# A two-block model on one core: fused mask and maximum, eight results per PSUM bank, x reloaded later

## The reference

```python
def dsa_attention(q, k, v, iq, ik, iw):       # 8 heads, per block of 128 queries
    ...
    logits = jnp.where(ok[:, :, None, :], logits, -jnp.inf)
    p = jax.nn.softmax(logits, axis=-1).astype(v.dtype)
    ...
def windowed_gqa(u, w_in, sink, w_out):       # 16 heads
    ...
        logits = logits - slopes[:, :, None, None] * dist
        logits = jnp.where(valid, logits, NEG_BIG)
        sink_col = jnp.broadcast_to(sink_l[None, :, :, None, None], logits.shape[:-1] + (1,))
        probs = jax.nn.softmax(jnp.concatenate([logits, sink_col], axis=-1), axis=-1)[..., :-1]
    ...
def second_block(x, p, ...):
    h = x
    for i in range(DEPTH_2):
        u = rms_norm_2(h, norm_g[i])
        ...                                    # y = windowed_gqa(u, ...), then y = mla(u, ...)
        h = h + y
        gate = jax.nn.sigmoid(rms_norm_2(h, ple_norm_g[i]) @ ple_w_gate[i])
        h = h + (p[i] @ ple_w[i]) * gate
    return rms_norm_2(h, final_norm_g)
```

## Time and profile before

| | |
|---|---|
| median of 3 runs | 2800.81 us (2798.86 to 2802.94) |
| the profiled execution | 2798.45 us, its span 2796.6 us |
| busy: PE, DVE, ACT, POOL | 2515.2, 1558.5, 594.7, 1602.1 us |
| chain that ended last | PE 77%, DVE 12%, DMA 3%, issue 2%, ACT 2%, POOL 2% |
| sparse attention | 321 to 381 us |
| gelu stage with gates | 792 to 1176, without them to 1282 |
| down stage | 1285 to 1963 |
| windowed attention | 2084 to 2212 |
| a_out, ple_w0, norm(3), ple_g0, norm(4) | 2223 to 2357 |
| latent attention | 2485 to 2644 |
| b_out, ple_w1, norm(5), ple_g1, norm(6) | 2653 to 2796 |

### The profile page before, as it was taken

The page is one execution under the profiler, slowest core; times in us unless marked ns, Lnnn a source line. Parts: engine busy times, 40 slices in busy tenths (PEclk is TensorE's granted clock), DMA queues, the critical chain, the costliest instruction groups (busy, mean ns, idle before and its releaser), DMA issues.

```text
span 2796.6 us, 38708 instructions
## 1 busy us (share of the span) xinstructions
PE 2515.2 (90%) x12856; PEld 1260.3 (45%) x12856; DVE 1558.5 (56%) x2823; ACT 594.7 (21%) x1243; POOL 1602.1 (57%) x1048
## 2 busy tenths in 40 slices
PE   3767788999999999978999999999898888989987
PEld 1423443444455555433444444444355533557633
DVE  6498583699967777505952222250218836555525
ACT  1111221111122222201111111110125322245412
POOL 4535435799976767659976666660560157830053
PEclk7878898999999999989999999999999999999998
DMA  6216312354446587577765555560220022310021
GB/s 228 98 44 215 118 38 80 113 150 143 146 147 199 179 249 246 166 217 254 261 220 204 201 204 201 204 224 15 84 83 1 9 75 68 106 53 1 9 75 38
DMA packets 189252, 375.45 MB, mean 134 GB/s; under 512 B 13536, under 2 KB 79200, under 8 KB 189152
## 3 DMA queue, kind: packets, MB, share of 16 engines
q1 hardware_dynamic: 119696, 332.64, 35.8%
q10 hardware_dynamic: 69456, 41.49, 5.0%
HBM read 302.77 MB, written 71.30 MB: 134 GB/s over the span
## 4 chain that ended last, share of the span: by engine, by line
PE 77%; DVE 12%; DMA 3%; issue 2%; ACT 2%; POOL 2%; ACTq 1%; SPq 0%; DVEq 0%; POOLq 0%
PE ps L624 65%; PE ps L714 3%; PE ps L734 3%; PE ps L840 2%; PE ps L723 2%; DMA arena<-ada_w 2%; DVE arena L1280 2%; PE ps L672 1%; ACTq L1097 1%; DVE arena L1384 1%; DVE arena L1383 1%; DVE spare L1190 1%; DVE arena L1245 1%; ACT arena L1016 1%; DVE arena L1218 1%
## 5 line engine op out<-in xcount | busy, mean ns | idle before, releaser
L624 PE MATMUL ps<-hT,parts 128*128 128x512 f16 x4800 | 1070.3, 383 | 66.1 <-DVE hT L1198 29.6
L573 POOL TENSOR_SCALAR parts<-ring 128x1024 f16<-128x1024 f32 x261 | 297.9, 1141 | 955.3 <-PE ps L624 890.0
L624 PEld LDWEIGHTS ps<-hT,parts 128*128 128x128 f16 x4800 | 466.5, 98 | 642.0 <-issue 43.3
L624 PE MATMUL ps<-arena 128*128 128x512 f16 x3072 | 666.2, 380 | 8.4 <-DVE arena L1544 8.4
L576 POOL TENSOR_TENSOR parts<-ring,parts 128x1024 f16<-128x1024 f32 x261 | 577.2, 2212 | 21.7
L624 PEld LDWEIGHTS ps<-arena 128*128 128x128 f16 x3072 | 300.9, 98 | 374.5 <-issue 15.0
L1539 DVE TENSOR_TENSOR arena<-arena 128x512 f32<-128x512 f32 x128 | 149.7, 1170 | 451.6 <-DMA arena<-gate_mem 447.8
L574 POOL TENSOR_SCALAR ring<-ring 128x1024 f32<-128x1024 f32 x261 | 306.6, 1175 | 0.0
L594 POOL TENSOR_TENSOR arena<-ring,arena 128x1024 f16<-128x1024 f32 x128 | 283.6, 2215 | 10.6
L592 POOL TENSOR_SCALAR arena<-ring 128x1024 f16<-128x1024 f32 x128 | 148.2, 1158 | 169.7 <-PE ps L624 169.7
L624 PE MATMUL ps<-arena,parts 128*128 128x512 f16 x876 | 199.8, 389 | 49.4 <-POOL parts L576 34.3
(11 more groups left out here) (169 smaller groups left out, 2414.6 us busy)
## 6 DMA issues: line engine op xcount, KB each, us to landing
ring<-w SPq DMA_DIRECT2D x133, 512.0 KB, 3.3
ring<-u SPq DMA_DIRECT2D x128, 512.0 KB, 3.9
ring<-v SPq DMA_DIRECT2D x128, 512.0 KB, 3.4
act_mem<-spare SPq DMA_DIRECT2D x128, 256.0 KB, 4.0
gate_mem<-arena ACTq DMA_DIRECT2D x4, 8192.0 KB, 42.0
arena<-act_mem SPq DMA_DIRECT2D x128, 256.0 KB, 3.6
arena<-gate_mem SPq DMA_DIRECT2D x128, 256.0 KB, 3.8
arena<-ada_w SPq DMA_DIRECT2D x48, 512.0 KB, 4.8
```

Of the source, the lines that this page charges most:

```text
L573: G.tensor_scalar(dst[:, 0, :], src, WS, 1.0, ALU.mult, ALU.mult).then_inc(scaled, 1)
L624: ins = [T.matmul(out_, a, b, start=start and j == 0, stop=stop and j == 2) for j, (a, b) in enumerate(((lhs[0], rhs[0]), (lhs[0], rhs[1]) ...
```

## The change

In the attention (all three kinds):

- mask and maximum are one VectorE instruction with an accumulator. It writes the negated logits and their minimum; the exp is then taken with scale -1. In the windowed kind the logits come already divided by the head's slope (the table `steep`, in the copy of a_q), the instruction multiplies by the slope again, and the negated sink is the minimum's starting value.
- the results of eight units lie side by side in one PSUM bank, and VectorE scales all eight at once; maxima, sums and sinks have a column for each of the eight. Values wait for a scaling only in the first unit of eight, for that of sixteen units back. The sinks' exponentials are done for eight units at once.

x is reloaded behind the last gelu. Beyond that, norms 1 and 3 to 6 have their parts moved into the stage ahead, two blocks behind it; in norms 3 and 5 the last two parts lie behind the second and third block of ple_w0 or ple_w1, and ScalarE's copies of that stage are spread over the norm. Norms 4 and 6 square into `aq`, as `hT` is still being read. A one-element root ahead of the last square loads the table early.

```diff
             def values(u):
                 ...
-                    if u0 + u >= 2:
-                        pe.wait_ge(o_ready, u0 + u - 1)
+                    if u % EIGHT == 0 and u0 + u >= 2 * EIGHT:
+                        pe.wait_ge(o_ready, (u0 + u) // EIGHT - 1)
+                    at = place(un) * 64
...
-            features("a_out", in_parts(az), lambda k: pe.wait_ge(turned_read, t_a + k + 1))
-            features("ple_w0", in_parts(pT), lambda k: pe.wait_ge(p_ready, k + 1))
-            norm(3)
-            features("ple_g0", hr, h_need(3))
-            norm(4)
+            features("a_out", in_parts(az), lambda k: pe.wait_ge(turned_read, t_a + k + 1), behind(3, 2))
+            features("ple_w0", in_parts(pT), lambda k: pe.wait_ge(p_ready, k + 1),
+                     lambda m: norm_part(3, KC - 3 + m) if m in (1, 2) else None)
+            features("ple_g0", hr, h_need(3), behind(4, 2))
+            last_parts(4, 2)
...
+            def square(n, k, need):
+                if k == KC - 1:
+                    own.do(A.activation(warm[:, n:n + 1], eps[:, 0:1], ACT.Sqrt))
+                need(k)
+                own.do(A.activation(squares_of(n)[:, k, :], xT[:, k, :], ACT.Square), squares)
...
-                    if un["kind"] == "window":
-                        own.do(A.activation(sm[:, 8 + u % 4:9 + u % 4],
...
+                    if un["kind"] == "window" and u % EIGHT == EIGHT - 1:
+                        act.wait_ge(sink_shifted, u // EIGHT + 1)
+                        own.do(A.activation(eight_sinks(u), eight_sinks(u), ACT.Exp), sink_exps)
...
+            gelus(AT_GATES + S // GROUP, CHUNKS)
             act.dma_start(xT[:, :, :], x_park.rearrange("c p n -> p c n")).then_inc(x_back, 16)
-            gelus(AT_GATES + S // GROUP, CHUNKS)
...
-            take("a_q", lambda s, b: copy(aq[:, s, :], b, scale=0.125 / WS))
+            act.wait_ge(rows2_loaded, 16)
+            steep = ROWS2["steep"][0]
+            take("a_q", lambda s, b: copy(aq[:, s, :], b, scale=rows2[:, steep + s:steep + s + 1]))
...
+                for s in range(KC + 1):
+                    if s < KC:
+                        take(name, gate, s, s + 1)
+                    if s >= 1:
+                        square(n + 1, s - 1, of_sum)
...
                     elif un["kind"] == "window":
...
-                        own.link(V.scalar_tensor_tensor(out=soft_b[:, u % 2, 0:w], in0=rows2[:, at:at + w],
-                                                        scalar=-slope, in1=src, op0=ALU.mult, op1=ALU.add))
-                        src = soft_b[:, u % 2, 0:w]
-                    ins = V.tensor_reduce(nm, src, AX, ALU.max, negate=True)
...
+                        own.do(V.tensor_tensor_reduce(out=soft_b[:, u % 2, 0:w], in0=src, in1=rows2[:, at:at + w],
+                                                      scale=-slope, scalar=small_w[:, 48 + un["h"]:49 + un["h"]],
+                                                      op0=ALU.add, op1=ALU.min, accum_out=peak(un, u)), max_ready)
...
                 def normalise(u):
+                    if u % EIGHT != EIGHT - 1:
+                        return
...
-                    own.do(V.tensor_scalar(out_rows(un), ps[:, u % 2, 0:64], tot, None, ALU.mult), o_ready)
...
+                        own.do(V.tensor_tensor(out_.rearrange("p (e d) -> p e d", d=64),
+                                               src.rearrange("p (e d) -> p e d", d=64), by, ALU.mult), o_ready)
```

More of the change, by code:

```diff
@@ L452, in soft_buffers, with peak, eight_peaks, total_at @@
             return soft_w, probs_w, probsT_w, small_w
+        def peak(un, u):
+            n = (u // EIGHT % 2) * EIGHT + place(un) + (32 if un["kind"] == "sparse" else 0)
+            return soft_buffers(un["kind"])[3][:, n:n + 1]
+        def eight_peaks(u):
+            n = (u // EIGHT % 2) * EIGHT
+            return small_w[:, n:n + EIGHT]
+        def total_at(un, u):
+            return (u // EIGHT % 2) * EIGHT + {"sparse": 48, "window": 16, "latent": 64}[un["kind"]]
+        def total(un, u):
+            n = total_at(un, u) + place(un)
+            return soft_buffers(un["kind"])[3][:, n:n + 1]
+        def eight_totals(un, u):
+            n = total_at(un, u)
+            return soft_buffers(un["kind"])[3][:, n:n + EIGHT]
+        def eight_sinks(u):
+            n = 32 + (u // EIGHT % 2) * EIGHT
+            return small_w[:, n:n + EIGHT]
         block = ctx.enter_context(nc.Block())
@@ L647, in features @@
                     last.then_inc(summed, 1)
+                    if after is not None:
+                        after(m)
             def tokens(name, lhs, need=None):
@@ L678, in norm, with behind, last_parts @@
                 for k in range(KC):
+                    norm_part(n, k)
+            def behind(n, lag):
+                return lambda m: norm_part(n, m - lag) if lag <= m < KC + lag else None
+            def last_parts(n, lag):
+                for k in range(KC - lag, KC):
                     norm_part(n, k)
@@ L980, in copy, with norm @@
                 return A.activation(dst, src, ACT.Copy, scale=scale)
-            def norm(n, need, shift_of=None):
-                for k in range(KC):
-                    need(k)
-                    own.do(A.activation(hT[:, k, :], xT[:, k, :], ACT.Square), squares)
+            def square(n, k, need):
[3 more added lines that the diff above has]
+                own.do(A.activation(squares_of(n)[:, k, :], xT[:, k, :], ACT.Square), squares)
+            def norm(n, need=None, shift_of=None, between=None):
+                if need is not None:
+                    for k in range(KC):
+                        square(n, k, need)
+                if between is not None:
+                    between(-2)
                 act.wait_ge(norm_sum, n + 1)
@@ L1124, in _, with embedded @@
             attention(units_window(), U_WINDOW)
-            take("ple_w0", lambda s, b: copy(ple[:, s, :], b))
             def ple_gate(name, n):
-                norm(n, x_from("a_out" if n == 3 else "b_out"))
+                def embedded(k):
+                    first, last = {-2: (0, 3), -1: (3, 6), 1: (6, 7), 2: (7, 8)}.get(k, (0, 0))
+                    take("ple_w0" if n == 3 else "ple_w1", lambda s, b: copy(ple[:, s, :], b), first, last)
+                norm(n, x_from("a_out" if n == 3 else "b_out"), between=embedded)
                 def gate(s, b):
@@ L1133, in gate, with of_sum @@
                     return A.activation(gate_t[:, s % 2, :], b, ACT.Sigmoid, scale=1.0 / WS)
-                take(name, gate)
+                def of_sum(k):
+                    act.wait_ge(x_ready, (0 if name == "ple_g0" else KC) + k + 1)
+                for s in range(KC + 1):
[3 more added lines that the diff above has]
+                        square(n + 1, s - 1, of_sum)
             ple_gate("ple_g0", 3)
-            norm(4, lambda k: act.wait_ge(x_ready, k + 1))
+            norm(4)
             take("b_c", lambda s, b: copy(lat[:, s, 0:512], b))
@@ L1731, in lay_out @@
     gap = np.abs(np.arange(3 * P)[None, :] - P - np.arange(P)[:, None]).astype(np.float32)
-    dist = np.where(gap <= WINDOW, gap, np.float32(FAR))
+    dist = np.where(gap <= WINDOW, -gap, np.float32(-FAR))
+    steep = np.empty((P, 8), np.float32)
+    for s_ in range(8):
+        for half_ in range(2):
+            h_ = (2 * (s_ // A_G) + half_) * A_G + s_ % A_G
+            steep[half_ * 64:half_ * 64 + 64, s_] = 0.125 / WS * 2.0 ** (8.0 * (h_ + 1) / A_H)
     half = ROPE // 2
```

98 lines of the change are left out of this document (62 added, 36 removed).

## The result

The change makes the kernel faster: 2723.38 us (median; 2722.78 to 2724.32) against 2799.89, a ratio of 0.9725, 95% interval 0.9708 to 0.9742. The forecast was 2733.0. The profiled execution took 2722.95 us with a span of 2721.0, so 75.6 us less span than before; the sum of the forecast had 67.8.

What follows compares the result with a forecast made beforehand. PE was taken as the bound, losing time to waits in gelus, attention and norms. Terms 24.6 + 21 + 5 + 3 + 15 - 0.8 = 67.8 us gave 2730.6 profiled, 2733 median; own range 2724 to 2744, wider range 2723 to 2751.

Steps and rivals of the forecast that it cites:

- PE's floor of 1.79 us: Windowed attention, three key blocks: PE's own time of 1.79 us a unit becomes the bound, above the loop's 1.70.
- root and reciprocal are hidden by what is left of ple_w0: Norms before ple_g0 and ple_g1: both paths to the next stage make 17.5 us, against 25.1 before.
- Reload, -24.6: Gelu stage: reloading x behind the last gelu removes ScalarE's 30.77 us issue and gains 24.6 us, from 16 to 25.
- Rival 2: Reload holds ScalarE 30.8 us again, ahead of the down stage's first copy; whole gain lost, 2758 us; chance 0.06.
- Windowed attention, -21: Fused mask and maximum, sink's exponential out of the unit: 21 us less, from 15 to 26.
- Sparse attention, -5: One reduction leaves the loop and scaling blocks no maximum: some 0.2 a unit, 5 us less, from 2 to 7.
- Latent attention, -3: Only the scaling per unit goes, the maximum is unchanged: 3 us less, from 0 to 4.5.
- Norms before ple_g0 and ple_g1, -15: Norm parts moved into the stage ahead gain 7.6 us at each of two places: 15 us, from 11 to 16.
- Rival 3: Slower: fused instruction costs the same at any width; 2877 us at the disturbed 3.13, 2765 at 1.28; chance 0.02.
- Norms after them, +0.8: Norms after ple_g0 and ple_g1: PE gains nothing from the moved parts, each norm costs 0.4 us more.
- Rival 1: Fusing buys nothing on VectorE: one instruction takes as long as the two, 0.84 and 1.11 us; 2750 us; chance 0.09.
- Rival 4: More than forecast: groups of eight cost nothing, latent and norms at their best ends; 2724 us; chance 0.07.

Runs made afterwards that it cites:

- e1: Kernel before with only the fused mask-and-maximum instruction in windowed and sparse attention; scaling and sink exponential stay per unit: 2772.98 us, ratio 0.990.
- e3: Kernel before with only the reload of x moved behind the last gelu: 2777.27 us, ratio 0.9915.
- e8: Kernel before with the reload of x moved behind the fourth of the sixteen last gelus: 2787.81 us, ratio 0.9956.
- e9: Changed kernel with the windowed attention's mask and maximum only on each unit's first 128 columns: 2722.8 us, ratio 0.9725.
- e4: Changed kernel with the parts of norm(3) and norm(5) one block behind the squares instead of two: 2722.58 us, ratio 0.9721.
- e2: Changed kernel with mask and maximum back in separate VectorE instructions, three windowed and two sparse: 2754.1 us, ratio 0.9833.
- e5: Changed kernel with GpSimd cutting no tile while VectorE writes the normalised x, for norms 1, 2, 3 and 5: 2710.76 us, ratio 0.968.
- e7: Changed kernel with norm(4) and norm(6) put back behind ple_g0 and ple_g1 as before: 2724.87 us, ratio 0.9735.

## Why the prediction was off, step by step

The sign and the places were right; the gain was 75.6 us of span where the sum had 67.8. Three steps failed: PE's floor of 1.79 us in the windowed units (its own pace is 1.64 to 1.65, and the loop's 1.71 is what came), 0.2 us a unit in the sparse part (0.25 by e1), and "root and reciprocal are hidden by what is left of ple_w0" (PE waits 1.58 us there). The first two made the sum too small by 2.9 and 3.1 us, the third too large by 1.3 at each of two norms. Term by term:

- **Reload, -24.6: right** (-24.66), and so was the reason: the length of the issue is the store's that is ahead of it in the queue (e3, e8). Rival 2 fell: there was no store left to wait for. Taking the gain from GpSimd's starts instead of PE's gap (24.65, not 22.56) was the right choice. The 2.1 us between them, the long first tile of the forecast, go with TensorE's clock behind the stop: 0.50 from 1197 to 1207 and 0.77 from 1207 to 1217.
- **Windowed attention, -21: mis-sized by 3.3.** The units with two blocks gained 60.0 - 49.2 = 10.8 us, and the forecast had 12.8 + 0.8 - 2.8 = 10.8. The miss is in the units with three blocks: 13.5 gained where 11.8 - 1.2 = 10.6 stood. The loop had given 1.70 a unit, which is what came (1.71), and I then put PE's "own 1.79" on top of it. That number was read between two sparse scores as a place "where nothing waits", but the loop ran there too: PE's weight loads, which those rows don't show, stood for 0.44 us behind exp ahead of the turn at 351.78. e9 has PE at 1.645. 32 x (1.79 - 1.71) = 2.6 of the 2.9 us. The 0.3 a group for scaling a bank didn't show. That the units with two blocks came out at 10.8 as forecast is in part luck: a group costs them some 0.2 us and not 0.7, and their first units ran at the low clock, which took 2.3 us (49.2 us in after, 46.9 in e4, where it was high).
- **Sparse attention, -5: mis-sized by 4.3.** I had read the reduction as 0.4 to 0.7 us for two units, took 0.2 a unit, the low end, and took end effects off. By the loop's own arithmetic it is 0.58 / 2 = 0.29 a unit with three blocks; e1 shows 8.1 us for 32 units, 0.25 each, all from the fused instruction. "VectorE no longer stands in a unit's scaling" is worth 0.2 us in all (e2). Another 1 us or so is TensorE's clock, below.
- **Latent attention, -3: right in kind** (-3.9), from the scaling alone, since e2 has all of it.
- **Norms before ple_g0 and ple_g1, -15: the step "root and reciprocal are hidden by what is left of ple_w0" failed** by 1.58 us each time. I took the 6.40 us from root to matmul from a trace in which GpSimd stood still, waiting for PE (it started again at 2294.09, after PE). Moved under ple_w0, the products meet GpSimd's cutting, and root to matmul takes 8.02 us. Rival 3 put just such a disturbance by GpSimd on the fused instruction, where GpSimd rests; the norms, where it works, had none. With GpSimd held (e5) the stretch before ple_g0 takes 72.88 us, 8.0 less than before, and the 7.6 of the forecast is there. The change gained 6.3 us at norm(3). At norm(5) the table has 8.0, but the norm's part of that is 6.3 too: 2725.99 - 2700.89 = 25.10 before and 2650.11 - 2635.62 = 14.49 after, less 4.29 for five parts in b_out. The other 1.7 is the clock at the start of b_out.
- **Norms after them, +0.8: right** (+0.7 in the table, 0.4 of it theirs by e7).
- **Rival 1** (fusing buys nothing) and **rival 3** fell with the first row: 0.62 and 0.48 us, to the hundredth what had been taken, so that the price does go with the width. The Trainium skill, "VectorE: DVE Perf Modes", section "Rules for kernel authors", has fusing as no gain in speed but for the number of instructions; here one for two or three is 0.62 us instead of 1.34. **Rival 4** was the nearest: its time, 2724, is what came, though not by its road. Its terms add up to some 74.3 us, which makes 2724 of the profiled execution and 2726.5 of the median; the norms and the latent part were not at their best ends, and the sparse part, which it left at 5, gave 9.3.

## What to carry over

Where two units circle between engines, add up one engine's part of the loop from start to start and halve the difference: it gave the pairs of units with three blocks in e1, e2 and after within 0.03 us, and it fails where an engine's own work is longer, as in e9 (3.15 by the loop, 3.29 measured). A floor for the busiest engine has to come from a place where it is held by nothing, or be added up from its instructions; two starts in another loop are no floor. And a duration read while a neighbour rests holds only while it rests: before moving VectorE's work under another stage, look at what GpSimd does there, and let it wait if it is ahead anyway. An equal total can hide an effect: e9's was that of after, with 4.5 us less in the windowed part.
